# Delta rule of a hybrid decoder block: the triangular solve works on the matrix and the right-hand side together

## What is computed

```python
kb = kc * bc[..., None]
a_mat = jnp.where(strict, jnp.einsum('bnhid,bnhjd->bnhij', kb, kc) * decay, 0.0)
t_mat = lax.linalg.triangular_solve(a_mat, eye, left_side=True, lower=True, unit_diagonal=True)
u = jnp.einsum('bnhij,bnhjd->bnhid', t_mat, vc * bc[..., None])
w = jnp.einsum('bnhij,bnhjd->bnhid', t_mat, kb * jnp.exp(gc)[..., None])
...
def step(state, inp):
    v_new = u_n - jnp.einsum('bhcd,bhde->bhce', w_n, state)
    o_n = jnp.einsum('bhcd,bhde->bhce', qd_n, state) + jnp.einsum('bhij,bhje->bhie', qk_n, v_new)
    state = state * gl_n[..., None, None] + jnp.einsum('bhcd,bhce->bhde', kd_n, v_new)
```

## Time and profile before

| | us |
|---|---|
| median of 3 runs (lowest, highest) | 2660.43 (2660.03, 2661.71) |
| the profiled execution, its own time | 2660.74 |
| its span in the trace | 2658.8 |
| busy: PE, DVE, ACT, POOL | 2612.6, 1812.4, 999.5, 336.7 |

### The profile page before, as it was taken

One profiled execution on the slowest core, in us unless ns is written; L12 is line 12 of the kernel. 1 busy time (PEld: TensorE's weight loads), 2 busy tenths in 40 slices (PEclk: granted clock), 3 DMA queues, 4 the chain that ended last, 5 costly groups with the idle time before them and its releaser, 6 DMA issues.

```text
span 2658.8 us, 43837 instructions
## 1 busy us (share of the span) xinstructions
PE 2612.6 (98%) x17358; PEld 2382.7 (90%) x17358; DVE 1812.4 (68%) x1715; ACT 999.5 (38%) x1016; POOL 336.7 (13%) x342
## 2 busy tenths in 40 slices
PE   8999999999999999999989999999999999999998
PEld 7999988888889977888879999999999998888886
DVE  4444555555553234558888888888888888888898
ACT  4443322222222232223354444444444444333334
POOL 5000034444442500110000000000000000000000
PEclk9999999999999999999999999999999999999999
DMA  4333323233333334779343444544454449866462
GB/s 140 100 90 93 86 82 93 83 91 85 88 91 95 107 91 153 242 264 329 128 148 124 154 157 148 178 151 156 148 181 150 154 150 344 275 198 219 162 203 102
DMA packets 346856, 400.86 MB, mean 151 GB/s; under 512 B 11625, under 2 KB 300562, under 8 KB 345618
## 3 DMA queue, kind: packets, MB, share of 16 engines
q1 hardware_dynamic: 287122, 335.39, 40.1%
q10 hardware_dynamic: 59664, 64.51, 7.1%
HBM read 328.02 MB, written 71.84 MB: 150 GB/s over the span
## 4 chain that ended last, share of the span: by engine, by line
PE 91%; DVE 3%; issue 2%; DMA 2%; ACT 1%; POOL 1%; SPq 0%; DVEq 0%; ACTq 0%; POOLq 0%
PE psum L2102 34%; PE psum L2420 10%; PE psum L2421 10%; PE psum L2422 10%; PE psum L2395 6%; PE psum L2397 6%; PE psum L2396 6%; PE psum L2256 2%; DMA dn_raw<-in_w_ffn_down 1%; PE psum L2262 1%; PE psum L2051 1%; PE psum L2079 1%; DMA w_raw<-in_w_proj_a 1%; PE psum L2335 1%; PE psum L2240 0%
## 5 line engine op out<-in xcount | busy, mean ns | idle before, releaser
L2102 PE MATMUL psum<-hn_hi,w_hi 128*128 128x264 f32 (+1 forms) x1600 | 450.6, 330 | 0.0
L2102 PE MATMUL psum<-hn_lo,w_hi 128*128 128x264 f32 (+1 forms) x1600 | 449.4, 330 | 0.0
L2102 PE MATMUL psum<-hn_hi,w_lo 128*128 128x264 f32 (+1 forms) x1600 | 448.6, 329 | 0.0
L1370 DVE TENSOR_TENSOR w_lo<-w_raw,w_hi 128x1024 fp32r<-128x1024 f32 x144 | 189.4, 1317 | 259.3 <-ACT w_hi L926 258.9
L926 ACT ACTIVATE w_hi<-w_raw 128x1024 fp32r<-128x1024 f32 x144 | 152.2, 1058 | 415.7 <-PE psum L2102 389.1
L2102 PEld LDWEIGHTS psum<-hn_hi,w_lo 128*128 128x128 f32 x1600 | 268.5, 188 | 22.8
L2102 PEld LDWEIGHTS psum<-hn_lo,w_hi 128*128 128x128 f32 x1600 | 268.8, 188 | 22.4 <-issue 0.7
L2102 PEld LDWEIGHTS psum<-hn_hi,w_hi 128*128 128x128 f32 x1600 | 268.8, 188 | 22.2 <-issue 0.2
L2395 PE MATMUL psum<-dn_hi,act_hl 128*128 128x512 f32 x616 | 240.9, 391 | 2.7 <-DVE dn_lo L1689 1.8
L2396 PE MATMUL psum<-dn_lo,act_hl 128*128 128x512 f32 x616 | 240.3, 390 | 0.0
L2397 PE MATMUL psum<-dn_hi,act_hl 128*128 128x512 f32 x616 | 240.2, 390 | 0.0
(11 more groups left out here) (353 smaller groups left out, 6276.0 us busy)
## 6 DMA issues: line engine op xcount, KB each, us to landing
w_raw<-in_w_in SPq DMA_DIRECT2D x144, 512.0 KB, 3.9
ffn_raw<-in_w_ffn_gate SPq DMA_DIRECT2D x44, 1024.0 KB, 7.1
ffn_raw<-in_w_ffn_up SPq DMA_DIRECT2D x44, 1024.0 KB, 6.5
dn_raw<-in_w_ffn_down SPq DMA_DIRECT2D x32, 1024.0 KB, 8.2
act_hl<-act_dram SPq DMA_DIRECT2D x56, 512.0 KB, 9.1
act_dram<-comb_hi ACTq DMA_DIRECT2D x22, 896.0 KB, 4.2
act_dram<-comb_lo ACTq DMA_DIRECT2D x22, 896.0 KB, 6.2
out_raw<-in_w_out SPq DMA_DIRECT2D x16, 1024.0 KB, 9.9
```

The lines of the kernel that those rows point to most:

```text
L1370: dve.tensor_tensor(wlo[s][:], raw[s][:], whi[s][:].bitcast(F32), ALU.subtract).then_inc(S["lo_ready"], 1)
L2102: ins = pe.matmul(o, lhs, r, start=kt == 0 and i == 0, stop=kt == 4 * n_chunks - 1 and i == 2)
```

## The change

The inverse is no longer built. Each level now acts at once on the matrix W and the right-hand side R, which lie beside each other in one tile `wr` (128 x 2 x 4 x 128): (W, R) = (W, R) - X (W, R), where X is the turned W times a fixed mask `levels`. After the last level R is `v_new` itself.

- The six products of levels 0 to 5 are four matmuls of 256 columns in place of 128. The last level takes R alone, from 64 rows, and its product is subtracted from 64 rows. The step that applied the inverse (L2269) and ScalarE's copy of its result (L1033) are gone.
- VectorE's update is one operation over 1024 columns per level for levels 0 to 5 (before: 512). X is one operation of 512, as before; the last one covers 64 rows.
- GpSimd's operations per level (`kept`, masks, `strict`) are gone, with their constants; beta goes into the matrix through small factors that VectorE computes, and the copies for the next half stand before the levels.
- The product k by (state, q, k) is one matmul of 384 columns per head in step 1. It waits for the square of q. The product q by state moves to step 4, behind the transposes of N. The transposes of level 5 cover 64 x 64.
- The first W is a copy of the turned N out of PSUM by ScalarE, which stands behind its four scaled copies of q by state.
- Two `sem_inc` on a semaphore that nobody waits for stand before the 64-row matmuls.

The diff, cut (the tiles' new names and places, GpSimd's constants, the small factors on VectorE and the renamed operations behind the levels are left out):

```diff
@@ -211,7 +211,13 @@
         v_at = kv_at + HEADS * TOK * 4
 
         tmp_at = top[0]
-        B = [place(f"gdn{i}", [P, GH, P]) for i in range(14)]
+        sqk = place("state_q_k", [P, 3, HEADS, P])
+        state, q_in, k_in = (sqk[:, i] for i in range(3))
+        v_in, kd, pt, rows_d = (place(name, [P, GH, P]) for name in ("v_in", "kd", "pt", "rows_d"))
+        wr = place("w_r", [P, 2, GH, P])
+        W, R = wr[:, 0], wr[:, 1]
+        qo, ko = place("qo", [P, GH, P]), place("ko", [P, GH, P])
...
-                    pool.wait_ge(S["z_ready"], (LEVELS + 1) * v + l + 1)
-                    pool.tensor_tensor(kept[:], B[11][:], over_heads(keep[:, l, :]), ALU.mult).then_inc(S["z_kept"], 1)
-                    if l + 2 < LEVELS:
...
                 act.wait_ge(S["qkv_turned"], 3 * v + 1)
-                act.activation(B[12][:], bank(0), ACT.Square).then_inc(S["q_squared"], 1)
+                act.activation(qo[:], bank(5), ACT.Square).then_inc(S["q_squared"], 1)
                 act.wait_ge(S["qkv_turned"], 3 * v + 2)
-                act.activation(B[13][:], bank(1), ACT.Square).then_inc(S["k_squared"], 1)
...
                 yield
                 act.wait_ge(S["norms_a"], 2 * v + 1)
-                act.wait_ge(S["s_products"], 2 * v + 2)
+                act.wait_ge(S["q_products"], v + 1)
                 act.wait_ge(S["staged"], 4 * v + 4)
                 for b in range(GH):
-                    act.activation(B[12][:, b, :], bank(0)[:, b, :], ACT.Copy, scale=heads_half(hf, D_BEGIN)[:, b:b + 1]) \
+                    act.activation(qo[:, b, :], bank(0)[:, b, :], ACT.Copy, scale=heads_half(hf, D_BEGIN)[:, b:b + 1]) \
                         .then_inc(S["qs_ready"], 1)
+                act.wait_ge(S["n_turned"], v + 1)
+                act.activation(W[:], bank(1), ACT.Copy).then_inc(S["w_ready"], 1)
                 yield
                 for _ in range(14):
                     yield
-                act.wait_ge(S["vn_product"], v + 1)
-                act.activation(B[10][:], bank(3), ACT.Copy).then_inc(S["vn_ready"], 1)
-                yield
...
+                dve.tensor_tensor(X[:], nt[:], over_heads(levels[:, 0, :]), ALU.mult).then_inc(S["x_ready"], 1)
+                dve.wait_ge(S["vb_ready"], v + 1)
                 dve.wait_ge(S["nbeg_ready"], v + 1)
                 for b in range(GH):
-                    dve.scalar_tensor_tensor(B[0][:, b, :], bank(5)[:, b, :], nbeg[:, b:b + 1],
-                                             B[6][:, b, :], ALU.mult, ALU.add).then_inc(S["rhs_ready"], 1)
-                yield
...
+                    dve.scalar_tensor_tensor(R[:, b, :], k_product(KS)[:, b, :], nbeg[:, b:b + 1], v_in[:, b, :],
+                                             ALU.mult, ALU.add).then_inc(S["rhs_ready"], 1)
                 yield
                 for l in range(LEVELS):
-                    dve.wait_ge(S["z_kept"], LEVELS * v + l + 1)
-                    dve.wait_ge(S["z_product"], LEVELS * v + l + 1)
-                    dve.tensor_tensor(B[11][:], kept[:], bank(1), ALU.subtract).then_inc(S["z_ready"], 1)
+                    dve.wait_ge(S["level_product"], LEVELS * v + l + 1)
+                    if l == 0:
+                        dve.wait_ge(S["rhs_ready"], GH * v + GH)
+                    dve.wait_ge(S["w_ready"], LEVELS * v + min(l, LEVELS - 2) + 1)
+                    if l < LEVELS - 1:
+                        both_w = wr[:].rearrange("p w h c -> p h w c")
+                        dve.tensor_tensor(both_w, both_w, level_both, ALU.subtract).then_inc(S["w_ready"], 1)
+                    else:
+                        dve.tensor_tensor(R[PH:P], R[PH:P], level_banks(1)[PH:P], ALU.subtract).then_inc(S["r_ready"], 1)
                     yield
...
-                        dve.tensor_tensor(XB[(l + 1) % 2][:], bank(2), mask_buf[(l + 1) % 2][:], ALU.mult) \
+                        dve.wait_ge(S["w_turned"], (LEVELS - 1) * v + l + 1)
+                        rows = slice(0, P if l < LEVELS - 2 else PH)
+                        dve.tensor_tensor(X[rows], bank(1)[rows], over_heads(levels[:, l + 1, :])[rows], ALU.mult) \
                             .then_inc(S["x_ready"], 1)
                         yield
                 yield
...
+                pe.wait_ge(S["q_squared"], v + 1)
                 for i in range(GH):
-                    ins = pe.matmul(bank(3)[:, i, :], B[8][:, i, :], B[8][:, i, :], start=True, stop=True)
-                ins.then_inc(S["kk_done"], 1)
-                for i in range(GH):
-                    ins = pe.matmul(bank(4)[:, i, :], B[8][:, i, :], B[7][:, i, :], start=True, stop=True)
-                ins.then_inc(S["kq_done"], 1)
-                yield
-                pe.wait_ge(S["q_squared"], v + 1)
-                for j, to in ((8, 5), (7, 0)):
-                    for i in range(GH):
-                        ins = pe.matmul(bank(to)[:, i, :], B[j][:, i, :], state[:, h0 + i, :], start=True, stop=True)
-                    ins.then_inc(S["s_products"], 1)
+                    ins = pe.matmul(PS[:, 2 + i, 0:3 * P].rearrange("p (w c) -> p w c", w=3), k_in[:, h0 + i, :],
+                                    sqk[:, :, h0 + i, :], start=True, stop=True)
+                ins.then_inc(S["k_products"], 1)
+                yield
                 yield
                 yield
                 pe.wait_ge(S["nt_ready"], v + 1)
                 pe.wait_ge(S["vb_ready"], v + 1)
                 for i in range(GH):
-                    ins = pe.transpose(bank(2)[:, i, :], B[10][:, i, :], ident[:])
+                    ins = pe.transpose(bank(1)[:, i, :], nt[:, i, :], ident[:])
                 ins.then_inc(S["n_turned"], 1)
-                yield
                 pe.wait_ge(S["kd_ready"], v + 1)
+                for i in range(GH):
+                    ins = pe.matmul(bank(0)[:, i, :], q_in[:, h0 + i, :], state[:, h0 + i, :], start=True, stop=True)
+                ins.then_inc(S["q_products"], 1)
+                yield
+                pe.wait_ge(S["rhs_ready"], GH * v + GH)
+                pe.wait_ge(S["pt_ready"], FREE["pt_ready"] + v + 1)
                 for l in range(LEVELS):
-                    x = XB[l % 2]
                     pe.wait_ge(S["x_ready"], LEVELS * v + l + 1)
-                    pe.wait_ge(S["z_ready"], (LEVELS + 1) * v + l + 1)
+                    pe.wait_ge(S["w_ready"], LEVELS * v + l + 1)
+                    if l == LEVELS - 1:
+                        pe.sem_inc(S["last_level"], 1)
                     for i in range(GH):
-                        ins = pe.matmul(bank(1)[:, i, :], x[:, i, :], B[11][:, i, :], start=True, stop=True)
-                    ins.then_inc(S["z_product"], 1)
+                        if l < LEVELS - 1:
+                            b = 2 * P * (i % 2)
+                            ins = pe.matmul(PS[:, 4 + i // 2, b:b + 2 * P].rearrange("p (w c) -> p w c", w=2), X[:, i, :],
+                                            wr[:, :, i, :], start=True, stop=True)
+                        else:
+                            ins = pe.matmul(level_bank(i, 1), X[0:PH, i, :], R[0:PH, i, :], start=True, stop=True)
+                    ins.then_inc(S["level_product"], 1)
                     yield
                     if l < LEVELS - 1:
-                        pe.wait_ge(S["z_ready"], (LEVELS + 1) * v + l + 2)
+                        pe.wait_ge(S["w_ready"], LEVELS * v + l + 2)
+                        if l == LEVELS - 2:
+                            pe.sem_inc(S["last_level"], 1)
                         for i in range(GH):
-                            ins = pe.transpose(bank(2)[:, i, :], B[11][:, i, :], ident[:])
-                        ins.then_inc(S["z_turned"], 1)
+                            if l < LEVELS - 2:
+                                ins = pe.transpose(bank(1)[:, i, :], W[:, i, :], ident[:])
+                            else:
+                                ins = pe.transpose(bank(1)[0:PH, i, PH:P], W[PH:P, i, 0:PH], ident[PH:P, PH:P])
+                        ins.then_inc(S["w_turned"], 1)
                         yield
-                pe.wait_ge(S["z_ready"], (LEVELS + 1) * (v + 1))
-                pe.wait_ge(S["rhs_ready"], GH * v + GH)
-                pe.wait_ge(S["pt_ready"], FREE["pt_ready"] + v + 1)
-                for i in range(GH):
-                    ins = pe.matmul(bank(3)[:, i, :], B[11][:, i, :], B[0][:, i, :], start=True, stop=True)
-                ins.then_inc(S["vn_product"], 1)
-                yield
-                pe.wait_ge(S["vn_ready"], v + 1)
+                yield
+                pe.wait_ge(S["r_ready"], v + 1)
                 pe.wait_ge(S["qs_ready"], GH * v + GH)
                 for i in range(GH):
-                    ins = pe.matmul(bank(0)[:, i, :], B[4][:, i, :], B[10][:, i, :], start=True, stop=True)
+                    ins = pe.matmul(bank(0)[:, i, :], pt[:, i, :], R[:, i, :], start=True, stop=True)
```

More of the change, by code:

```diff
@@ L56 @@
 META_LEVELS = 4
[L57 removed]
+N_CONSTS = 16 + 3 * LEVELS
```

(5 more changed lines are left out.)

150 lines of the change are left out of this document (66 added, 84 removed).

## The result

| | before | after |
|---|---|---|
| median of 4 runs each, on one chip (lowest, highest) | 2660.52 (2660.03, 2661.71) | 2699.28 (2699.06, 2701.20) |
| the profiled execution, its own time | 2660.74 | 2699.45 |
| its span | 2658.8 | 2697.7 |

The change makes the kernel slower: the ratio is 1.0146, with an interval of 1.0134 to 1.0159. It costs 38.8 us between the medians where 33.9 were forecast, and 2699.28 lies inside the range of 2687 to 2704. So the direction and the main term were right; what has to be explained is where 5 us more came from.

The account below looks back on a forecast made before the run. TensorE was taken to bound the loop, busy without gaps in a half, so every added column costs its full time. Terms (a) to (i) summed to +33.9 us on 2660.74, stated as 2694 us, range 2687 to 2704.

Parts of the forecast that it names:

- (a): Six level products per half get 256 columns at 107 ns per added 128 columns and record: +41.1 us.
- (h): First level's product waits for ScalarE's copy into W, 0.14 us late per half: +1.1 us.
- (b): The step that applied the inverse goes, saving 0.90 us per half: -7.2 us.
- (c): Head of the half: same columns, one change between gate matmuls and fp32 products fewer: -0.4 us.
- (d): Level 5's transposes take 64 columns and not 128, saving 0.15 us per half: -1.2 us.
- (e): Two changes per half between 128 and 64 rows, and two `sem_inc`, 0.1 us per half: +0.8 us.
- (f): VectorE's 1024-column update stays covered by TensorE's eight gate matmuls, with 0.29 us to spare: 0 us.
- (g): Late X in one level per half goes with GpSimd's per-level operations, 0.13 us per half: -1.0 us.
- (i): First half: old stall goes, -4.4 us; step 1's wait for the square of q plus low clock, +5.1 us.
- columns hidden: Rival: weight loads hide the level products' second 128 columns, so their cost vanishes: 2653 us; chance 0.05.
- late update: Rival: VectorE's update, drawn out to 1.88 us, delays the transposes 0.37 us in 48 levels: 2712 us; chance 0.07.
- first half's wait hidden: Rival: ScalarE reaches the square of q sooner, so the first half's wait costs nothing: 2689 us; chance 0.08.

Follow-up runs that it names:

- the second profile: The changed kernel run again, unaltered, as base for the small edits on the same chip: 2698.93 us, ratio 1.0144.

## Why the prediction was right, and where it was off

The forecast half was 65.8 us and the measured one 66.36. In eight halves the terms (a) to (h) were to add 33.2 us and added 37.6, so 4.4 of the error of 4.9 stands there. By terms:

- **(a) Columns, +41.1.** Right. The half is 5.03 longer with the columns than without them, 40.2 in all.
- **(b) The apply step, -7.2.** Right. In the kernel with full rows the last product and what stood with it take 4.55 us to the next step where before it was 5.46, 0.91 less. ScalarE's copy behind it gave nothing, as forecast.
- **(c) The head's products, -0.4.** Not resolved. With (h) the head costs 0.17 more per half, and the entry to the first level alone 0.26, so some 0.09 was saved elsewhere in it; 0.05 was forecast.
- **(d) Level 5's transposes, -1.2, and (e) the switches of rows, +0.8.** Together -0.4 forecast, +3.5 measured: most of the whole error. The step that was off is (e). The transposes of 64 columns did get cheaper inside their block, as (d) said: the second of four starts at 583.73 and, in the trace, the last at 583.84, 0.056 us from record to record, where those of 128 columns stand 0.109 apart; that is 0.16 per half. But the block still takes 0.34 us (583.64 to 583.98), as the full one does (560.10 to 560.46), because its edges take the gain back: its last record is 0.14 ahead of the gate matmul, where a full block has 0.03, and its first is 0.08 ahead of the second. These edges cost 0.14 together. With the 0.28 of the product and twice 0.08 ahead of the blocks, the two changes of rows cost about 0.6 us per half and not 0.1, a little over the bound of 0.5. The price had come from dividing a block of ten records of 32 rows by ten, which spreads over the records what its edges cost: in that trace the records inside stand 0.11 apart, the last one 0.19 ahead of the next matmul.

The block as a whole, then once more from its second record on:

```profile
583.64 0.41 PE L2267 MATMUL psum<-ident,w_r 64*64 64x64 f32 x4
583.98 0.50 PE L2098 MATMUL psum<-hn_lo,w_hi 128*128 128x512 f32 x1
...
583.73 0.33 PE L2267 MATMUL psum<-ident,w_r 64*64 64x64 f32 x3
```

- **(f) The update, 0.** Right, and its strided output did not draw it out: 1220 to 1223 ns in all 48, against 1215 for the like operation.
- **(g) Late X, -1.0.** The products after that level begin on time now; 0.11 of the 0.13 per half came, 0.9.
- **(h) The first level's wait, +1.1.** The mechanism was right, the size was not: 0.32 per half in place of 0.14, 2.6 in all. The sum of ScalarE's times had no room for what lies between the copy's end and the product's start (0.14 here, 0.05 assumed), nor for the first product's slower step.
- **(i) The first half, -4.4 and +5.1.** The gap was forecast at 3.36 and measured at 3.35 and 3.34. The low clock behind it, 1.74, was there in the second profile (1.69) and not in the first. The half was to last 70.9; it lasted 69.94 and 71.64.
- **What no term held.** In the first profile the loop began 1.1 us later, with a low clock near 44 us that the profile of the kernel before did not have, and the stretch behind the loop was 0.9 longer. Both are matters of one execution: in the second profile the loop began 0.3 later than before, and the stretch behind it was 0.6 shorter, though the wait at L2394 was as long as in the first (2.8 and 2.6 us, against 1.0 before). That wait is therefore not what the 0.9 is.

So (d) and (e) are off by +3.9 and (h) by +1.5, (a) by -0.9 and (c) by -0.3: 4.2 of the 4.4 per eight halves. The 0.5 left of the whole error is smaller than what one execution differs from the next. That 2699.28 lies in the range owes something to this: the terms too small were partly made up by a term (a) too large. The rivals: the first (columns hidden) fell with the kernel without the second columns; the second (late update) needs more work than VectorE has, as the kernel with the added operation shows; the third (first half's wait hidden) fell with the gap of 3.35. One thing in the first is true: at 128 columns a record takes about as long as its load, 0.11 us, so narrower products with the same weights gave nothing.

## What to carry to other kernels

Where TensorE has no gaps, as in this loop, and its matmuls have 128 columns or more, a transformation is judged by columns added against columns taken away: here 24 x 128 columns per half came in to save 4 x 128 and a great deal of work on an engine that nobody waited for. Beside such a stream even the small print costs: a matmul with other rows than its neighbours, or a copy queued behind four others, is worth a few tenths of a microsecond each time. The one-off gaps in the first pass of this loop depended on the order of work in a queue: moving GpSimd's masks ahead of one operation took about 2.5 us off the kernel before, where the whole rewrite added 38.8.

## What the runs showed of the hardware

- A full fp32 matmul on TensorE cost two records of 107 ns at 128 columns and 213 to 215 ns at 256 (0.43 us from start to start per product of 256). Below 128 columns it got no cheaper with weights of 128 x 128: 64 and 128 columns together took as long as twice 128, and the loads came every 0.11 us. Transposes of 64 x 64, whose weights are 64 x 64 too, stood 0.056 us apart against 0.109 for 128 x 128.
- Eight records of 64 rows between full ones took 1.09 us and not 0.81, all of it at the edges of the block, and the loads did not run ahead of them. With the transposes of 64 rows the change cost 0.44 us per half, net of what the narrower transposes saved.
- Behind a gap of TensorE the granted clock fell to half, 1.2 GHz, for some microseconds in some executions and not in others. Behind the gap of 3.35 us it did in 7 of the 9 profiles that have it; behind the 1.5 us that the later k products left in none of 3; behind 2.65 in the kernel before, but not behind the 1.35 of its variant. Near 43 us, behind a gap of 2.6, it did in 10 of 13 profiles, both of the changed kernel among them. The fourteenth, with the later k products, fell at 31.8 already, behind a gap of 1.8 that all have and that set off no fall in the others. Each of these falls cost 1.5 to 1.7 us, but for that last one, 0.2, because the next wait shrank from 2.6 to 1.3. Such a fall can't be forecast for one profile, only its likelihood.
